# A two-layer decoder step on one core: pipelined final norm in both arms of the branch, and four edits to the attention

## What is computed

```python
def _layer(x, l, ...):
    # mixing: input projection, pooling, conv, recurrence, output projection
    x = x + mixed @ P['w_out'][l]
    x = x + mem_attend(rmsnorm(x, P['norm_mem'][l]), mk, mv, P['w_mq'][l], P['w_mo'][l])
    hn = rmsnorm(x, P['norm_ffn'][l])
    x = x + (swiglu(hn, ...) if l % 2 == 0 else moe(hn, ...))   # moe: top 2 of 8 experts
def mem_attend(xn, k, v, wq, wo):        # 4 heads of 256, 256 memory tokens
    q = xn @ wq
    p = softmax(q k^T / 16)
    return (p v) @ wo
y = rmsnorm(x, P['final_norm'])          # after layer 1
```

## Time and profile before

| | us |
|---|---|
| median of 3 runs (lowest, highest) | 1116.09 (1115.86, 1120.1) |
| the profiled execution's own time | 1118.94 |
| its span, first to last instruction | 1117.1 |
| PE busy | 1061.1 (95%) |
| DVE busy | 780.0 (70%) |
| ACT busy | 652.5 (58%) |
| POOL busy | 21.4 (2%) |
| DMA, mean over the span | 244 GB/s |

### The profile page before, as it was taken

The page is one execution under the profiler, slowest core; times in us unless marked ns, Lnnn a source line. Parts: engine busy times, 40 slices in busy tenths (PEclk is TensorE's granted clock), DMA queues, the critical chain, the costliest instruction groups (busy, mean ns, idle before and its releaser), DMA issues.

```text
span 1117.1 us, 19890 instructions
## 1 busy us (share of the span) xinstructions
PE 1061.1 (95%) x7693; PEld 1002.8 (90%) x7693; DVE 780.0 (70%) x1080; ACT 652.5 (58%) x900; POOL 21.4 (2%) x40
## 2 busy tenths in 40 slices
PE   5999999999999998999999879999999999999994
PEld 4999987899999998999986869899999999999983
DVE  5597753576555556589734469898889889888873
ACT  5667543564434444575534457777777767776751
POOL 0001000000000000001010000000000000000000
PEclk8999999999999999999999989999999999999997
DMA  9454569946555554443579619898989898898941
GB/s 372 162 180 145 163 246 350 365 155 201 176 184 177 182 185 147 163 149 136 170 270 370 243 54 359 316 366 288 364 294 359 289 337 310 317 341 308 351 189 41
DMA packets 64275, 272.99 MB, mean 244 GB/s; under 512 B 7328, under 2 KB 7584, under 8 KB 63552
## 3 DMA queue, kind: packets, MB, share of 16 engines
q1 hardware_dynamic: 62352, 264.33, 66.2%
q0 software_dynamic: 1408, 7.12, 1.7%
q10 hardware_dynamic: 432, 0.38, 0.1%
HBM read 265.83 MB, written 5.98 MB: 243 GB/s over the span
## 4 chain that ended last, share of the span: by engine, by line
PE 74%; DVE 13%; ACT 6%; DMA 4%; issue 2%; SPq 1%; DVEq 0%; ACTq 0%
PE bank L650 11%; PE bank L652 11%; PE bank L651 11%; PE bank L647 11%; PE bank L648 10%; PE bank L649 10%; DMA ring<-dense 4%; DVE wl L1507 3%; ACT wh L1107 2%; DVE rstd L1501 2%; DVE sq L1518 1%; PE bank L674 1%; PE bank L784 1%; PE bank L956 1%; PE bank L957 1%
## 5 line engine op out<-in xcount | busy, mean ns | idle before, releaser
L1507 DVE TENSOR_TENSOR wl<-ring,wh 128x1024 fp32r<-128x1024 f32 x170 | 206.2, 1224 | 181.4 <-ACT wh L1107 179.9
L647 PE MATMUL bank<-xh,wh 128*128 128x264 f32 x928 | 270.5, 292 | 13.3 <-DVE xl L1523 10.0
L1107 ACT ACTIVATE wh<-ring 128x1024 fp32r<-128x1024 f32 x170 | 178.3, 1056 | 155.0 <-PE bank L649 119.1
L1776 DVE TENSOR_TENSOR wl<-ring,wh 128x1408 fp32r<-128x1408 f32 x144 | 232.5, 1622 | 51.0 <-ACT wh L1368 50.8
L648 PE MATMUL bank<-xl,wh 128*128 128x264 f32 x928 | 266.0, 287 | 0.0
L649 PE MATMUL bank<-xh,wl 128*128 128x264 f32 x928 | 265.7, 286 | 0.0
L1368 ACT ACTIVATE wh<-ring 128x1408 fp32r<-128x1408 f32 x141 | 194.7, 1381 | 50.4 <-PE bank L652 49.0
L647 PEld LDWEIGHTS bank<-xh,wh 128*128 128x128 f32 x928 | 177.2, 191 | 21.4 <-issue 16.1
L651 PE MATMUL bank<-wh,xl 128*128 128x352 f32 (+4 forms) x560 | 184.7, 330 | 0.0
L648 PEld LDWEIGHTS bank<-xl,wh 128*128 128x128 f32 x928 | 177.8, 192 | 0.0
L649 PEld LDWEIGHTS bank<-xh,wl 128*128 128x128 f32 x928 | 177.0, 191 | 0.0
(11 more groups left out here) (256 smaller groups left out, 1726.2 us busy)
## 6 DMA issues: line engine op xcount, KB each, us to landing
ring<-experts SPq DMA_DIRECT2D x192, 704.0 KB, 6.0
ring<-dense SPq DMA_DIRECT2D x234, 512.0 KB, 4.1
o_k<-kv POOLq DMA_DIRECT2D x2, 1024.0 KB, 4.4
o_v<-kv POOLq DMA_DIRECT2D x2, 1024.0 KB, 7.5
x<-xT SPq DMA_DIRECT2D x2, 528.0 KB, 4.9
o_y<-sq SPq DMA_DIRECT2D x4, 264.0 KB, 2.1
gatew<-gate_w POOLq DMA_DIRECT2D x2, 512.0 KB, 8.2
mem<-memT SPq DMA_DIRECT2D x1, 1024.0 KB, 13.3
```

What stands on the lines that cost most here:

```text
L647: mm(out, s_hi, m_hi, start=start, stop=False)
L1107: A(parts(k)[0], raw(u), ACT.Copy).then_inc(hi_ready, 1)
L1507: V.tensor_tensor(w_lo, raw(u), w_hi.bitcast(F32), ALU.subtract)\
L1776: V.tensor_tensor(w_lo, eraw(jj % ESLOTS), w_hi.bitcast(F32), ALU.subtract)\
```

## The change

The branch is turned round (`count <= CAP` first), and each arm ends with its own `finish`. For one pass, `finish` on PE is: chunks 0 to 3 of the last scatter after `D0` alone, chunks 4 to 7 after `D1`, each followed by a product that sums the squares of a chunk four behind, then the last four of those. ACT squares each chunk as soon as it is added, scales 4 chunks by the gain in place (`final_gain`), takes the root, scales the other 4. DVE inverts, then makes y for chunks 0, 1, 2, 4, 6; POOL makes 3, 5, 7, both as one product of two SBUF operands. SP stores in the same pairs. The root's function table is loaded by a dummy activation between `D0` and `D1` of each last expert. The loads of the count move: on ACT and DVE ahead of the first pass, on PE into the last pair (`fetch_count`, before the last transposes `T2`). The wait for `ident_ready` moves from before the pass to `turn_scatter`.

In attention: the splitters go 4 rather than 5 units ahead while queries are made; `sample_values` 2 and 3 stand behind `prompt_values` 4 and 5; on DVE `pz` is made before `top(1, 1)`, `o8` before the low part of m = 6, and the first low part of `mo` no longer stands before `o8`; POOL's stores wait for chunk 0 of the output projection.

```diff
@@ SP
-            for c in range(0, KC, 2):
-                sp.wait_ge(y_ready, c + 2)
+            sp.wait_ge(y_ready, 2)
+            sp.dma_start(o_y[:, 0:2, :], xn[:, 0:2, :]).then_inc(y_written, 16)
+            for i, c in enumerate((2, 4, 6)):
+                sp.wait_ge(y_ready, i + 3)
+                sp.wait_ge(y_pool_ready, i + 1)
                 sp.dma_start(o_y[:, c:c + 2, :], xn[:, c:c + 2, :]).then_inc(y_written, 16)
@@ PE
                 for m in range(KC):
                     prompt_values(m)
-                sample_values(2)
-                sample_values(3)
+                    if m in (4, 5):
+                        sample_values(m - 2)
...
                 pe.wait_ge(gcol_lo_ready, p + 1)
+                pe.wait_ge(ident_ready, 1)
...
+            def finish(ps):
+
+                num, before = ps.after, block_of(ps.last, "b")
+
+                def square_sum(m):
+                    b = take_bank(ps.final_sum) if m == 0 else bank(ps.final_sum)
+                    pe.wait_ge(fsq_ready, m + 1)
+                    i = mm(b[:, 0:T], ones[:, :], sq[:, m, :], start=(m == 0), stop=(m == KC - 1))
+                    if m == KC - 1:
+                        full(i, ps.final_sum)
+
+                wait_read(pe, *before("D0"))
+                for c in range(4):
+                    scatter_chunk(c, num)
+                wait_read(pe, *before("D1"))
+                for c in range(4, KC):
+                    scatter_chunk(c, num)
+                    square_sum(c - 4)
+                for m in range(4, KC):
+                    square_sum(m)
...
+                elif p == main.p0 + main.np - 1:
+                    fetch_count()
                 turn_hidden(num, 2)
...
-                scatter(ps.after, block_of(ps.last, "b"))
...
-            pe.wait_ge(ident_ready, 1)
             run_pass(main)
...
+            with pe.If(counted[0] <= CAP):
+                finish(main)
+            with pe.Else():
+                scatter(main.after, block_of(main.last, "b"))
                 run_pass(extra)
+                finish(extra)
@@ ACT
-                        S.upto(behind("mq", l, m, 5, start("mo", l)))
+                        S.upto(behind("mq", l, m, 4, start("mo", l)))
...
+                    if last and u == 0:
+                        A(small[:, 95:96], eps[:, 0:1], ACT.Sqrt)
...
+            def finish(ps):
+                for m in range(KC):
+                    wait_read(act, *ps.after(f"C{m}"))
+                    A(sq[:, m, :], x[:, m, :], ACT.Square).then_inc(fsq_ready, 1)
...
+                for m in range(4):
+                    final_gain(m)
+                wait_full(act, ps.final_sum)
+                A(rms[:, 0, :], bank(ps.final_sum)[:, 0:T], ACT.Sqrt, bias=eps[:, 0:1], scale=1.0 / D).then_inc(frms_ready, 1)
+                for m in range(4, KC):
+                    final_gain(m)
@@ DVE
-                        S.upto(behind("mq", l, c, 5, start("mo", l)))
+                        S.upto(behind("mq", l, c, 4, start("mo", l)))
...
-                for t in range(2):
-                    top(t, 1)
+                top(0, 1)
...
                 signal(pz_ready)
+                top(1, 1)
...
                 for m in range(KC):
+                    if m == 6:
+                        n = tiles[("pvs", l)]
+                        wait_full(dve, n)
+                        read(V.tensor_copy(o8, bank(n)[:, 0:HD]), n)
                     n = tiles[("pv", l, m)]
...
-                S.upto(start("mo", l) + 1, 0)
-                n = tiles[("pvs", l)]
-                wait_full(dve, n)
-                read(V.tensor_copy(o8, bank(n)[:, 0:HD]), n)
...
+            def finish():
+
+                dve.wait_ge(frms_ready, 1)
+                V.reciprocal(rstd[:, 0, :], rms[:, 0, :]).then_inc(frstd_ready, 1)
+                dve.wait_ge(frstd_ready, 1)
+                for m in (0, 1, 2, 4, 6):
+                    dve.wait_ge(xf_ready, m + 1)
+                    V.tensor_tensor(xn[:, m, :], x[:, m, :], rstd[:, 0, :], ALU.mult).then_inc(y_ready, 1)
@@ POOL
                     wait_read(pool, tiles[key_tile(l, m)])
+                wait_full(pool, tiles[("mo", l, 0)])
                 pool.dma_start(o_k[l], kT).then_inc(kv_written, 16)
...
+            pool.wait_ge(frstd_ready, 1)
+            for m in (3, 5, 7):
+                pool.wait_ge(xf_ready, m + 1)
+                G.tensor_tensor(xn[:, m, :], x[:, m, :], rstd[:, 0, :], ALU.mult).then_inc(y_pool_ready, 1)
```

More of the change, by code:

```diff
@@ L209, in __init__ @@
             self.end = self.tail + len(TAIL)
+            self.final_sum = self.end
         def first(self, kind):
@@ L465, in trunk_kernel @@
         fsq_ready = sem("final_squares_ready")
-        fsum_ready = sem("final_sum_ready")
         frms_ready = sem("final_rms_ready")
+        frstd_ready = sem("final_rstd_ready")
+        xf_ready = sem("x_times_final_norm_ready")
         y_ready = sem("y_ready")
+        y_pool_ready = sem("y_of_gpsimd_ready")
         y_written = sem("y_written")
@@ L976, in scatter, with scatter_chunk @@
                 for c in range(KC):
-                    n, more = num(f"C{c}")
-                    b = take_bank(n, more)
-                    for side in range(2):
-                        s = scat[:, side * T:(side + 1) * T]
-                        f0 = side * D + c * P
-                        mm(b[:, 0:T], eoh[:, f0:f0 + P], s, start=(side == 0), stop=False)
-                        i = mm(b[:, 0:T], eol[:, f0:f0 + P], s, start=False, stop=(side == 1))
-                    full(i, n)
+                    scatter_chunk(c, num)
+            def scatter_chunk(c, num):
+                n, more = num(f"C{c}")
+                b = take_bank(n, more)
+                for side in range(2):
+                    s = scat[:, side * T:(side + 1) * T]
+                    f0 = side * D + c * P
+                    mm(b[:, 0:T], eoh[:, f0:f0 + P], s, start=(side == 0), stop=False)
+                    i = mm(b[:, 0:T], eol[:, f0:f0 + P], s, start=False, stop=(side == 1))
+                full(i, n)
+            def finish(ps):
[11 more added lines that the diff above has]
+                for c in range(4, KC):
+                    scatter_chunk(c, num)
+                    square_sum(c - 4)
+                for m in range(4, KC):
+                    square_sum(m)
             def turn_hidden(num, i3):
@@ L1066, in _, with fetch_count @@
                     wait_read(pe, tiles[("tk", l, t, hp)])
-            pe.wait_ge(ident_ready, 1)
+            counted = []
+            def fetch_count():
+                pe.wait_ge(route_ready, 1)
+                counted.append(pe.value_load(need[0:1, 0:1], min_val=0, max_val=T))
             run_pass(main)
-            pe.wait_ge(route_ready, 1)
-            count = pe.value_load(need[0:1, 0:1], min_val=0, max_val=T)
-            with pe.If(count > CAP):
+            with pe.If(counted[0] <= CAP):
+                finish(main)
+            with pe.Else():
+                scatter(main.after, block_of(main.last, "b"))
                 run_pass(extra)
-            with pe.Else():
-                pe.nop()
-            for m in range(KC):
-                pe.wait_ge(fsq_ready, m + 1)
-                i = mm(psum[0][:, 0:T], ones[:, :], sq[:, m, :], start=(m == 0), stop=(m == KC - 1))
-            i.then_inc(fsum_ready, 1)
+                finish(extra)
         @block.scalar
@@ L1962, in _ @@
                 elow(0, j)
+            dve.wait_ge(route_ready, 1)
+            count = dve.value_load(need[0:1, 0:1], min_val=0, max_val=T)
             run_pass(main)
-            count = dve.value_load(need[0:1, 0:1], min_val=0, max_val=T)
-            with dve.If(count > CAP):
+            with dve.If(count <= CAP):
+                finish()
+            with dve.Else():
                 run_pass(extra)
-            with dve.Else():
-                dve.nop()
-            dve.drain().then_inc(x_final, 1)
-            dve.wait_ge(frms_ready, 1)
-            link(V.reciprocal(rstd[:, 0, :], rms[:, 0, :]))
-            for m in range(KC):
-                k = VEC_FINAL + m
-                V.scalar_tensor_tensor(out=xn[:, m, :], in0=x[:, m, :], scalar=vec[:, k:k + 1], in1=rstd[:, 0, :], op0=ALU.mult,
-                                       op1=ALU.mult).then_inc(y_ready, 1)
+                finish()
         @block.gpsimd
```

18 lines of the change are left out of this document (9 added, 9 removed).

## The result

The kernel after takes 1109.2 us in the median of 6 runs (1106.08 to 1111.25), the kernel before 1115.97 beside it (6 runs): ratio 0.9936, interval 0.9909 to 0.9963. So it is faster, by 7 us, where 13.8 were forecast; 1109.2 lies 0.7 above the upper end of the range.

A forecast was written before the change was run, and what follows sets the result against it. Bound: a serial relay at the end with PE's sums mostly at the lower clock; PE's waits and loads in attention. End 8.8 + gather 1.6 + attention 3.4 = 13.8; median 1116.09 - 13.8 = 1102.3 us, range 1096.5 to 1108.5.

The forecast's parts named there:

- The root 9.0 earlier: End: sums interleaved with the scatter at full clock let the root begin at 1099.95 instead of 1108.96, 9.0 us earlier.
- Products: End: y's products split over DVE and POOL taking turns, 3.55 us, 0.2 worse than the 3.32 before.
- The jump behind the last instruction: End: each engine's jump over the other arm is covered by the final store but for about 0.3 us.
- First gather 1.6: First gather: PE waits only for the last token part, not the rounded identity, saving 1.6 us.
- Attention 3.4: Attention: fewer waits and earlier loads gain 2.2 us in layer 1 and 1.2 in layer 0, together 3.4.
- `pz` first: Attention: making `pz` ahead of `top(1, 1)` removes a wait of 0.46 us, the same taken for layer 0.
- The 0.85 behind the last prompt value: End of attention: the way to the projection takes some 2.7 us instead of 3.55, saving 0.85 on PE's path.
- they land earlier as far as slots are freed earlier: Attention loads: 6.7 of 43 us are gaps, and PE frees several slots 1.6 to 2.1 us sooner.
- the loads hold the projection: Rival, chance 0.20: loads hold the projection behind attention, so attention gives -1.6 to 0, time 1105.7 to 1107.3 us.
- The baseline: Whole kernel: the 13.8 us summed from one profile was subtracted from the median 1116.09, giving 1102.3.
- Stores instead of loads: Rival, chance 0.02: stores moved to the projection land late behind expert loads, DVE's first write waits; 1122 at 665.
- the new arm pays: Rival, chance 0.08: branch, final sums at 1.2 GHz or POOL's products cost 2 to 3 us each; two together 1107 to 1109.

The follow-up runs named there:

- attention with the gather: Kernel before with only the attention edits, the moved stores and the moved identity wait, end as before: 1116.21 us, ratio 1.0005.
- the end alone: Kernel after with attention, stores and the identity wait as in the kernel before: 1112.67 us, ratio 0.9963.
- light: Kernels before and after, PE's waits filled with unread matmuls, each unit of cached values loaded by a quarter only: 1106.97 and 1098.97 us.
- filled pair: Kernels before and after with unread matmuls in PE's waits, moved ahead of those waits into free banks: 1109.47 and 1104.9 us.
- sums alone filled: Kernel before with 18 unread matmuls in PE's wait ahead of the final sums, count fetched earlier, short arm following its compare: 1114.54 us, ratio 0.9976.
- jumps held: Kernel after with PE, ACT and DVE waiting for all stores of y to land before leaving the short arm: 1111.7 us, one run.

## Why the prediction was wrong, by its own steps

- **The root 9.0 earlier**: right, 8.9. The clock at 1.00, the interleaved sums and the root "some 7 to 8 us after the last projection matmul" came as written, and the branch of the new arm costs nothing that can be seen. Of the 8.9, 2.85 are the cold sums that a few spare matmuls give back in the kernel before too (14.03 instead of 16.85 from the last projection matmul to the root).
- **Products**: 3.55 with turns was forecast, 3.44 measured, 0.60 worse than DVE alone (forecast 0.75). The estimate from the Trainium skill's ratio (GPSIMD Engine Reference, section 3.1), 3.8 for the turns, was a little high; the direction of the Trainium skill's rule (section 4.1 there), against the split, was right.
- **The jump behind the last instruction, which the final store "covers ... but for about 0.3"**: failed in part. About 0.3 does lie behind the landing. But the cover is the store itself, and the fetches are DMA transfers beside it, which make it land later. From the root on, the end came out 1.3 longer, so it gave 7.6 in the pair of profiles instead of 8.8.
- **First gather 1.6**: 1.3 off PE's wait (5.96 to 4.64), and 1.3 from the end of the projection to the gather. Right in kind, a fifth too big.
- **Attention 3.4**: this is the step that failed, and in it the new order of the values with the loads behind it. 3.4 were forecast, nothing came (0.6 us slower by the ratio of attention with the gather, 1.0 faster to 2.0 slower). Its first part was right (0.96 and 1.64 of waits gone; the scores came 1.0 and 1.5 to 1.7 earlier), and without the new order 2.3 of it reach the projection. `pz` first gave nothing: a wait of 0.44 is left where 0.46 was the earlier trace rows. The 0.85 behind the last prompt value came (2.8 instead of 3.55), but "they land earlier as far as slots are freed earlier" failed: DMA was at 0.98 of its time, and the last values land 1.2 earlier where PE asks 3 earlier. So the two prompt values behind them cost what the rest had gained. It was the first rival, *the loads hold the projection*, that came: its mechanism, and nearly its price (1105.7 to 1107.3, to which the tail's 1.2 has to be added). It had 0.20; the best stretch of 407 GB/s was read as room for all 43 us.
- **The baseline**: subtracting from the median a sum made in one profile takes for granted that the two kernels draw alike. They don't quite: 12.9 in the pair, where the medians lie 7 apart; about 5.5 is the difference between the two draws, as far as like clock can tell.

Sum: 7.6 + 1.3 and about -1.6 for attention make the 7.3 found at like clock; the last term is what remains, not a measurement by itself. *Stores instead of loads* and *the new arm pays* did not come, apart from the tail.

Open: the end alone gave 4 us unfilled, with a mean clock of 0.982, although 6.68 us mostly at half clock had gone from its end. Its executions lose about as much elsewhere; why that kernel draws worse was not found. So the two parts, 4.1 and -0.6 by the ratios, don't add up to the 6.4 of the whole that ran with them, though the intervals (1.5 to 2.5 us to each side) leave room for it. And of the 3.4 between the light and the filled pair, 2.3 were not located.

## What to carry to other kernels

A profile is one execution: before a sum is set against a median, look at how the times of the runs go with the granted clock, and compare at like clock, unless the change itself takes work out of the lower clock. In a stage like this one, where DMA was busy for 0.93 to 0.98 of the time, work that was moved away from in front of a load's consumer turned into a wait for that load, and the stage ended where it had ended before. Cheap filling matmuls in PE's known waits can be worth as much as many edits (here 7 us of the kernel before), if they stand ahead of the wait and in a free bank; behind the wait the same filling made the kernel slower (1120.36).

## What was not expected of the hardware

- The lower clock is a matter of the execution: waits of 1.66 and 1.07 us ahead of the projection of layer 0 left PEclk at 1.00 (sums alone filled), waits of 1.54 and 0.98 at the same place in the first profile of before did not (0.83 over 204 to 214). Behind a wait of 2.11 32 matmuls of the sample values took 1.91, behind one of 2.30 in another kernel 3.39; 32 of the sample scores took 1.93 behind 0.96 and 3.45 behind 2.35.
- One instruction fetch of 8 KB beside the data of 264 KB stores goes with landings of 2.6 to 3.5 us instead of 2.1 to 2.3 (after, the end alone; jumps held).
- DVE and POOL took turns on products of two SBUF operands: DVE's went from 0.43 to 0.96 beside POOL's 0.83 to 0.93.
